# The unit of attention and indexer keys of a hybrid decoder trunk, multiplied in plain float32

## The chip, the cores and the metric

The program runs on one core of one Trainium2 chip. The metric is the device time of one execution in microseconds (us). TensorE (PE) multiplies matrices, VectorE (DVE) and ScalarE (ACT) work element by element, GpSimd (POOL) does small things, SyncE (SP) issues nearly all DMAs. Each engine runs its own instructions in order; semaphores join them.

## The reference, cut to what matters

Two layers over 256 tokens of width 1024, all float32. Each has a mixer and then a channel part (a dense SwiGLU in layer 0, top-2-of-8 experts in layer 1). The mixer's input projection is cut into segments:

```python
proj = h @ w_in
aq, ak, av, iq, ik, iw, bq, bk, bv, bg, ba = jnp.split(proj, _split_points(), axis=-1)
y_a = dsa_attention(aq, ak, av, iq, ik, iw * IDX_HEADS ** -0.5)   # indexer, top-k keys, softmax
log_a = jax.nn.log_sigmoid(ba @ w_a2 + b_a) / GATE_TAU
o = gla(bq, bk, bv, log_a)                                        # gated linear attention
y = jnp.concatenate([y_a, rms_norm(o, gla_g) * silu(bg)], axis=-1) @ w_out
```

`ak` (64 wide) are the attention keys, `ik` (64) the indexer keys, `av` (64) the attention values, `iw` (8) the indexer's head weights. The change concerns these four.

## The kernel before, in words

The program is written by hand, one list of instructions for each engine (`block.sync`, `block.gpsimd`, `block.scalar`, `block.tensor`, `block.vector`), so the order in the source is the order on each engine.

**Units.** The input projection is loaded and multiplied in 12 units of up to 256 columns (`W_IN_UNITS`: BQ, BA, BK, IQ0, IQ1, KEYS, AQ0, AQ1, BV0, BV1, BG0, BG1), the output projection in 4 more. A unit of weights lands in one of four buffers `u_raw` (L419, issued by SP). The first two units (`PLAIN`) are multiplied as they are, in float32 (L984, L978), with `hfull`, the modulated tokens. The others are split: ACT copies the unit into `u_high` in the type float32r (`conv_unit`, L646), DVE subtracts that from the raw weights and writes the rest into `u_low` (`low_unit`, L1508), over the raw buffer; the tokens are split alike into `hT_H` and `hT_L`. `mm3` (L329 to L331) then makes each product out of three: high by high, low by high, high by low. There are three buffers `u_high`, taken in turn, so `conv_unit` waits until the unit three before has been multiplied.

**The unit KEYS** (number 5, `U_KEYS`) has 200 columns: `ak` and `ik` in columns 0 to 127, `iw` and `av` in 128 to 199. Only the first 128 are split (ACT L644, DVE L1506) and multiplied by `mm3`, 8 products of 128x256. The last 72 are multiplied in float32 by `mm4` (L932), which makes one product out of four column groups; these read the raw weights. ACT then copies the results out of PSUM (`evacuate`, L660 to L666); the copy of `iw` (L663) releases the indexer's products of queries and keys (`head_products`, L1034).

**Order around it.** On ACT: convert IQ1, `decay_in`, copy out BK, convert KEYS, `decay_out`, copy out IQ0, convert AQ0 (L646), `decay_keys` (L714, two exponentials of `kfac`), copy out IQ1, convert AQ1, copy out KEYS, then the indexer's relus (L753). On DVE: `decay`, `decay_keys` (L1595, L1598), the low part of KEYS (L1506), `decay_products` (L1607 to L1613; L1613 multiplies `kfac` and waits for the exponentials), the low parts of AQ0 and AQ1 (L1508), two rows of the conditioning matrix (`condition_rows`, L1495 and L1497), the indexer's sums (L1550, L1552), the selection by repeated maximum (L1566, L1567). On PE: BQ, BA, BK, IQ0, IQ1, KEYS, the indexer's products, the decay products (L932, L1081), AQ0, AQ1, the attention logits (L1034 with `akP`), and so on. On SP a unit's load waits until the unit four before has been multiplied; rows 66 and 67 (6 and 7 in layer 0) of the conditioning matrix and the load of BV1 wait for KEYS.

Of the kernel before, what the change touches and what calls it, by code (L numbers as in the profile page):

```python
# [17 lines left out]
F32 = mybir.dt.float32  # L18
# [56 lines left out]
PLAIN = 2  # L75
NSPLIT = NU - PLAIN
KW = 200
# [28 lines left out]
def hybrid_decoder(nc, x, c, w_in, w_a2, b_a, gla_norm_g, w_out, w_mod, b_mod, ln_g, ln_b,  # L106
# [3 lines left out]
    with ctx:  # L110
# [512 lines left out]
        def _(act):  # L623
# [11 lines left out]
            def conv_unit(l, u):  # L635

                act.wait_ge(w_ld[u % 4], unit_landed(l, u))
                if u >= PLAIN + 3:
                    act.wait_ge(s["proj"], l * NU + u - 2)
                elif l:  # L640
                    act.wait_ge(s["f_gu"], 2 * (STEPS - 1))
                dst, src = u_high[(u - PLAIN) % 3], u_raw[u % 4]
                if u == U_KEYS:
                    A(dst[:, :, 0:P], src[:, :, 0:P], ACT.Copy).then_inc(s["wH"], 1)  # L644
                else:
                    A(dst[:], src[:], ACT.Copy).then_inc(s["wH"], 1)  # L646

# [82 lines left out]
            def mixer(l):  # L730
# [9 lines left out]
                evacuate(l, U_BK)  # L740
                conv_unit(l, U_KEYS)
                decay_out(l)
# [182 lines left out]
        def _(pe):  # L925
# [45 lines left out]
            def project(l, u):  # L971
                b = bank[4 + u % 2]
                if u < PLAIN:
# [13 lines left out]
                    return  # L987
                WH, WL, W = u_high[(u - PLAIN) % 3], u_low[u % 4], u_raw[u % 4]
                pe.wait_ge(s["wL"], l * NSPLIT + u - PLAIN + 1)
                if u == PLAIN:  # L990
                    pe.wait_ge(s["hT_L"], 4 * l + 2)
                pe.wait_ge(s["evac"], l * NIN + u - 1)
                if u in (U_BV0, U_BV1, U_BG0, U_BG1):
                    for t in range(TT):
                        tok = slice(t * P, (t + 1) * P)
                        for kt in range(KT):
                            last = mm3(b[:, t * 256:(t + 1) * 256], hT_H[:, kt, tok], hT_L[:, kt, tok],
                                       WH[:, kt, :], WL[:, kt, :], kt == 0, kt == KT - 1)
                else:
                    for ct in range(1 if u == U_KEYS else 2):  # L1000
                        cc = slice(ct * P, (ct + 1) * P)
                        for kt in range(KT):
                            last = mm3(b[:, ct * T:(ct + 1) * T], WH[:, kt, cc], WL[:, kt, cc],
                                       hT_H[:, kt, :], hT_L[:, kt, :], kt == 0, kt == KT - 1)
                    if u == U_KEYS:
                        for t in range(TT):
                            for kt in range(KT):
                                last = mm4(b[:, T + t * 72:T + (t + 1) * 72], hfull[:, kt, t * P:(t + 1) * P], W[:, kt, P:KW],
                                           start=(kt == 0), stop=(kt == KT - 1))
                last.then_inc(s["proj"], 1)  # L1010

            def project_out(l, i, kts):

                u, v = NIN + i, W_OUT_ORDER[i]
                pe.wait_ge(s["wL"], l * NSPLIT + u - PLAIN + 1)
                WH, WL = u_high[(u - PLAIN) % 3], u_low[u % 4]
                for t in range(TT):
# [385 lines left out]
        def _(dve):  # L1403
# [97 lines left out]
            def low_unit(l, u):  # L1501

                dve.wait_ge(s["wH"], l * NSPLIT + u - PLAIN + 1)
                H, L, src = u_high[(u - PLAIN) % 3], u_low[u % 4], u_raw[u % 4]
                if u == U_KEYS:
                    V.tensor_tensor(L[:, :, 0:P], src[:, :, 0:P], H[:, :, 0:P].bitcast(F32), ALU.subtract).then_inc(s["wL"], 1)  # L1506
                else:
                    V.tensor_tensor(L[:], src[:], H[:].bitcast(F32), ALU.subtract).then_inc(s["wL"], 1)  # L1508

# [142 lines left out]
            def mixer(l):  # L1652
# [17 lines left out]
                decay_keys(l)  # L1670
                low_unit(l, U_KEYS)
                decay_products(l)
# [297 lines left out]
```

## Time and profile before

| | |
|---|---|
| median of 3 runs | 1322.58 us (1322.08 to 1323.61) |
| the profiled execution's own time | 1323.89 us |
| its span (first to last instruction) | 1322.2 us |
| mean granted TensorE clock | 0.975 of full speed |
| busy: PE, DVE, ACT | 1212.8, 552.1, 312.4 us |
| mixer of layer 1, from its transposes to its last product | 392.6 to some 523 us |

A profile shows one execution. Busy shares are means over stages with different limits: the experts of layer 1 (from about 555 us on) fill PE, while the mixers go back and forth between the engines. What a change in a mixer is worth is read from the waits of that place: which of the engines is waited for last.

### The profile page before, as it was taken

The numbers are of one execution on the slowest core, as the hardware profiler recorded it, in microseconds if no ns is written. First come the engines' busy times: TensorE is split into PE (matmuls) and PEld (weight loads), VectorE is DVE, ScalarE is ACT, GpSimd is POOL, SyncE is SP. The second block draws the span as 40 slices with busy tenths as digits, with TensorE's granted clock in tenths as the row PEclk, the third lists the DMA queues.
The fourth block names the chain that finished last, engine by engine and source line by source line (L and its number), as shares of the span: only waits on it lengthen the run. The fifth ranks groups of instructions, "written<-read, shape, count | busy, mean of one in ns | idle before, by whom it ended". The sixth has DMA issues, their size and how long they took to land.

```text
span 1322.2 us, 26435 instructions
## 1 busy us (share of the span) xinstructions
PE 1212.8 (92%) x11284; PEld 657.5 (50%) x11284; DVE 552.1 (42%) x841; ACT 312.4 (24%) x545; POOL 43.5 (3%) x84
## 2 busy tenths in 40 slices
PE   2988979999979887699999999999999999999996
PEld 1878867778858877423333333334333333333332
DVE  6898877777658997520021020020110210200224
ACT  0556133443236560220020020011110201200200
POOL 3100010000010000100000000000000000000001
PEclk9999979999989999799999999999999999999998
DMA  9954767899617549588999989989989989989850
GB/s 341 314 193 160 256 227 287 314 358 322 231 50 219 183 153 379 217 318 351 411 334 406 364 305 415 413 324 404 375 306 411 402 335 383 390 351 411 339 224 32
DMA packets 149083, 403.60 MB, mean 305 GB/s; under 512 B 19964, under 2 KB 71328, under 8 KB 137696
## 3 DMA queue, kind: packets, MB, share of 16 engines
q1 hardware_dynamic: 146720, 395.16, 79.9%
q0 software_dynamic: 2240, 6.68, 1.4%
q8 instruction: 92, 1.51, 0.5%
q14 instruction: 31, 0.25, 0.0%
HBM read 400.75 MB, written 1.05 MB: 304 GB/s over the span
## 4 chain that ended last, share of the span: by engine, by line
PE 67%; DVE 9%; issue 2%; DMA 1%; ACT 1%; POOL 0%; DVEq 0%; SPq 0%; ACTq 0%
PE bank L1284 34%; PE bank L1308 17%; PE bank L329 3%; PE bank L331 3%; PE bank L330 3%; PE bank L1318 2%; PE bank L1264 1%; DVE u_low L1508 1%; PE bank L1289 1%; DVE mod_acc L1497 1%; PE bank L1272 1%; DMA raw_u<-in_ffn_w_up_dram 1%; PE bank L1273 1%; PE bank L984 1%; DVE score L1567 1%
## 5 line engine op out<-in xcount | busy, mean ns | idle before, releaser
L1284 PE MATMUL bank<-raw_w,xg 128*32 128x512 f32 x4096 | 457.8, 593 | 1.1 <-issue 1.1
L1284 PEld LDWEIGHTS bank<-raw_w,xg 128*32 128x32 f32 x4096 | 126.7, 109 | 260.4 <-issue 258.2
L1308 PE MATMUL bank<-raw_w,heT 128*32 128x512 f32 x2112 | 232.9, 593 | 0.0
L1859 DVE TENSOR_TENSOR he<-he,bank 128x256 f32<-128x256 f32 x64 | 23.3, 417 | 384.5 <-ACT he L843 384.5
L1308 PEld LDWEIGHTS bank<-raw_w,heT 128*32 128x32 f32 x2112 | 66.9, 110 | 148.8 <-issue 147.6
L843 ACT ACTIVATE he<-bank 128x256 f32<-128x256 f32 (+1 forms) x72 | 21.4, 370 | 413.1 <-PE bank L1284 282.2
L1886 DVE SCALAR_TENSOR_TENSOR ycat<-bank,gate_tab,ycat 128x512 f32<-128x512 f32 x36 | 25.4, 747 | 184.7 <-PE bank L1273 182.8
L1497 DVE SCALAR_TENSOR_TENSOR mod_acc<-mod_row,c_act,mod_acc 128x1024 f32<-128x1024 f32 x70 | 89.9, 1284 | 9.6 <-DMA mod_row<-in_w_mod_dram 3.9
L329 PE MATMUL bank<-u_high,hT_H 128*128 128x256 f32 x256 | 75.1, 293 | 4.6 <-DVE u_low L1508 4.6
L331 PE MATMUL bank<-u_high,hT_L 128*128 128x256 f32 x256 | 72.8, 284 | 0.0
L330 PE MATMUL bank<-u_low,hT_H 128*128 128x256 f32 x256 | 72.7, 284 | 0.0
L329 PE MATMUL bank<-gu_H,hT_H 128*128 128x512 f32 x160 | 64.8, 405 | 0.0
L646 ACT ACTIVATE u_high<-u_raw 128x2048 fp32r<-128x2048 f32 x26 | 49.7, 1911 | 63.7 <-DMA u_raw<-in_w_in_dram 43.7
L331 PE MATMUL bank<-gu_H,hT_L 128*128 128x512 f32 x160 | 63.2, 395 | 0.0
L330 PE MATMUL bank<-gu_L,hT_H 128*128 128x512 f32 x160 | 63.1, 394 | 0.0
L1508 DVE TENSOR_TENSOR u_low<-u_raw,u_high 128x2048 fp32r<-128x2048 f32 x26 | 59.0, 2287 | 9.5 <-ACT u_high L646 9.3
L850 ACT ACTIVATE heT<-bank 128x512 f32<-128x512 f32 x24 | 14.3, 597 | 192.2 <-PE bank L1318 192.2
L1870 DVE TENSOR_TENSOR y_sum<-y_sum,bank 32x512 f32<-32x512 f32 x48 | 32.9, 686 | 62.1 <-ACT y_sum L867 61.6
L329 PEld LDWEIGHTS bank<-u_high,hT_H 128*128 128x128 f32 x256 | 49.1, 192 | 7.4 <-DVE u_low L1508 5.9
L329 PE MATMUL bank<-hT_H,u_high 128*128 128x256 f32 x176 | 50.6, 287 | 1.5 <-DVE u_low L1506 1.5
L331 PE MATMUL bank<-hT_H,u_low 128*128 128x256 f32 x176 | 49.6, 282 | 0.0
L330 PE MATMUL bank<-hT_L,u_high 128*128 128x256 f32 x176 | 49.5, 281 | 0.0
(292 smaller groups left out, 1497.8 us busy)
## 6 DMA issues: line engine op xcount, KB each, us to landing
raw_w<-in_moe_w_down_dram SPq DMA_DIRECT2D x88, 1024.0 KB, 8.3
raw_w<-in_moe_w_gate_dram SPq DMA_DIRECT2D x128, 512.0 KB, 7.3
raw_w<-in_moe_w_up_dram SPq DMA_DIRECT2D x128, 512.0 KB, 8.6
mod_row<-in_w_mod_dram SPq DMA_DIRECT2D x80, 512.0 KB, 6.6
raw_w<-in_moe_w_gate_dram SPq DMA_DIRECT2D x64, 384.0 KB, 3.8
raw_w<-in_moe_w_up_dram SPq DMA_DIRECT2D x64, 384.0 KB, 5.0
u_raw<-in_w_in_dram SPq DMA_DIRECT2D x20, 1024.0 KB, 7.8
raw_d<-in_ffn_w_down_dram SPq DMA_DIRECT2D x11, 1024.0 KB, 9.9
```

Of the source, the lines that this page charges most:

```text
L329: nc.tensor.matmul(out_ap, aH, bH, start=first, stop=False)
L330: nc.tensor.matmul(out_ap, aH, bL, start=False, stop=False)
L331: return nc.tensor.matmul(out_ap, aL, bH, start=False, stop=last)
L646: A(dst[:], src[:], ACT.Copy).then_inc(s["wH"], 1)
L1284: last = mm(bank[m // 4][32 * q:32 * q + 32, :].rearrange("s (m f) -> s m f", m=2), xg[:, i, k, 32 * g:32 * g + 32], W[:, :, a * 256:(a + ...
L1308: last = mm(bank[3 + g][32 * q:32 * q + 32, :], heT[:, i, at:at + 32], W[:, b, h * 512:(h + 1) * 512], start=(c == 0 and a == 0), stop=(c ...
L1318: last = nc.tensor.transpose(o, rows, ident[:])
L1497: last = V.scalar_tensor_tensor(out=acc, in0=row[:], scalar=c_act[:, k:k + 1], in1=acc, op0=ALU.mult, op1=ALU.add)
L1508: V.tensor_tensor(L[:], src[:], H[:].bitcast(F32), ALU.subtract).then_inc(s["wL"], 1)
L1859: last = V.tensor_tensor(he[:, b, :], he[:, b, :], bank[b][:, 256:512], ALU.mult)
L1870: last = V.tensor_tensor(a, a, bank[3 + g][64 * h + 32:64 * h + 64, :], ALU.add)
L1886: V.scalar_tensor_tensor(out=a, in0=bank[b][:], scalar=gate_tab[:, t, bass.ds(E, 1)], in1=a, op0=ALU.mult, op1=ALU.add).then_inc(s["m_acc" ...
```

## The change

KEYS is no longer split. ACT and DVE lose their two instructions for it in each layer, PE multiplies its first 128 columns in float32 from `u_raw` and `hfull`, and waits for the landing of the weights instead of for `u_low`. The remaining split units are numbered by their place in the list `SPLIT`, which sets which `u_high` buffer each takes and which product `conv_unit` waits for. The copies out of PSUM, the 72 other columns and all DMAs stay.

```diff
-NSPLIT = NU - PLAIN
+SPLIT = [u for u in range(PLAIN, NU) if u != U_KEYS]
+NSPLIT = len(SPLIT)
...
                 act.wait_ge(w_ld[u % 4], unit_landed(l, u))
-                if u >= PLAIN + 3:
-                    act.wait_ge(s["proj"], l * NU + u - 2)
+                if SPLIT.index(u) >= 3:
+                    act.wait_ge(s["proj"], l * NU + SPLIT[SPLIT.index(u) - 3] + 1)
                 elif l:
                     act.wait_ge(s["f_gu"], 2 * (STEPS - 1))
-                dst, src = u_high[(u - PLAIN) % 3], u_raw[u % 4]
-                if u == U_KEYS:
-                    A(dst[:, :, 0:P], src[:, :, 0:P], ACT.Copy).then_inc(s["wH"], 1)
-                else:
-                    A(dst[:], src[:], ACT.Copy).then_inc(s["wH"], 1)
+                dst, src = u_high[SPLIT.index(u) % 3], u_raw[u % 4]
+                A(dst[:], src[:], ACT.Copy).then_inc(s["wH"], 1)
...
                 evacuate(l, U_BK)
-                conv_unit(l, U_KEYS)
                 decay_out(l)
...
-                WH, WL, W = u_high[(u - PLAIN) % 3], u_low[u % 4], u_raw[u % 4]
-                pe.wait_ge(s["wL"], l * NSPLIT + u - PLAIN + 1)
+                if u == U_KEYS:
+                    W = u_raw[u % 4]
+                    pe.wait_ge(w_ld[u % 4], unit_landed(l, u))
+                    pe.wait_ge(s["evac"], l * NIN + u - 1)
+                    for kt in range(KT):
+                        mm(b[:, 0:T], W[:, kt, 0:P], hfull[:, kt, :], start=(kt == 0), stop=(kt == KT - 1))
+                    for t in range(TT):
+                        for kt in range(KT):
+                            last = mm4(b[:, T + t * 72:T + (t + 1) * 72], hfull[:, kt, t * P:(t + 1) * P], W[:, kt, P:KW],
+                                       start=(kt == 0), stop=(kt == KT - 1))
+                    last.then_inc(s["proj"], 1)
+                    return
+                WH, WL = u_high[SPLIT.index(u) % 3], u_low[u % 4]
+                pe.wait_ge(s["wL"], l * NSPLIT + SPLIT.index(u) + 1)
...
-                if u == U_KEYS:
-                    V.tensor_tensor(L[:, :, 0:P], src[:, :, 0:P], H[:, :, 0:P].bitcast(F32), ALU.subtract).then_inc(s["wL"], 1)
-                else:
-                    V.tensor_tensor(L[:], src[:], H[:].bitcast(F32), ALU.subtract).then_inc(s["wL"], 1)
+                V.tensor_tensor(L[:], src[:], H[:].bitcast(F32), ALU.subtract).then_inc(s["wL"], 1)
...
                 decay_keys(l)
-                low_unit(l, U_KEYS)
                 decay_products(l)
```

How the instructions stand now is shown at two places. First, PE at the unit KEYS of layer 0, before: the end of its products out of high and low parts (`u_high_185`, `u_low_182`; eight such triples), the 72 other columns (`32x72 x64`), and the indexer's products behind them.

```order
L329 MATMUL bank<-hT_H,u_high_185 128x256
L330 MATMUL bank<-hT_L,u_high_185 128x256
L331 MATMUL bank<-hT_H,u_low_182 128x256
L932 MATMUL bank<-u_raw_178,hfull 32x72 x64
L1034 MATMUL bank<-ikP,iqT 128x128 x8
L1034 MATMUL bank<-ikP,iqT 128x256 x8
L932 MATMUL bank<-qfP,kfac 32x2x32 x64
```

The same place in the changed kernel: the last product of IQ1, then KEYS from `hfull` and the raw weights.

```order
L330 MATMUL bank<-hT_H,u_high_187 128x256
L331 MATMUL bank<-hT_L,u_high_187 128x256
L332 MATMUL bank<-hT_H,u_low_181 128x256
L990 MATMUL bank<-hfull,u_raw_178 128x256 x8
L929 MATMUL bank<-u_raw_178,hfull 32x72 x64
L1038 MATMUL bank<-ikP,iqT 128x128 x8
L1038 MATMUL bank<-ikP,iqT 128x256 x8
L929 MATMUL bank<-qfP,kfac 32x2x32 x64
```

Of 24 instructions 8 are left, and they no longer read what DVE wrote; all behind them stands as it did.

Second, DVE in layer 0, from `decay_keys` to the low parts of AQ0 and AQ1, before:

```order
L1595 TENSOR_TENSOR kfac<-bT 128x1024
L1598 TENSOR_SCALAR kfac<-kfac 128x1024
L1506 TENSOR_TENSOR u_low_182<-u_raw_178,u_high_185 128x8x128
L1607 TENSOR_TENSOR qfP<-bqT,dec_117 64x2x256
L1608 TENSOR_TENSOR qxP<-bqT,dec_118 64x2x128
L1607 TENSOR_TENSOR qfP<-bqT,dec_117 64x2x256
L1608 TENSOR_TENSOR qxP<-bqT,dec_118 64x2x128
L1609 TENSOR_TENSOR kx<-kx,bkT 128x256
L1613 TENSOR_TENSOR kfac<-kfac,bkT 128x1024 x2
L1508 TENSOR_TENSOR u_low_183<-u_raw_179,u_high_186 128x2048
L1508 TENSOR_TENSOR u_low_184<-u_raw_180,u_high_187 128x2048
```

And in the changed kernel:

```order
L1596 TENSOR_TENSOR kfac<-bT 128x1024
L1599 TENSOR_SCALAR kfac<-kfac 128x1024
L1608 TENSOR_TENSOR qfP<-bqT,dec_117 64x2x256
L1609 TENSOR_TENSOR qxP<-bqT,dec_118 64x2x128
L1608 TENSOR_TENSOR qfP<-bqT,dec_117 64x2x256
L1609 TENSOR_TENSOR qxP<-bqT,dec_118 64x2x128
L1610 TENSOR_TENSOR kx<-kx,bkT 128x256
L1614 TENSOR_TENSOR kfac<-kfac,bkT 128x1024 x2
L1509 TENSOR_TENSOR u_low_183<-u_raw_179,u_high_185 128x2048
L1509 TENSOR_TENSOR u_low_184<-u_raw_180,u_high_186 128x2048
```

The subtraction of KEYS is gone and AQ0 takes the buffer `u_high_185`, which was that of KEYS; the order of the rest is the same.

## Rows read from the trace of the kernel before

**Rows 1.** The page, part 4: shares of the span in the chain of waits, by engine

```profile
PE 67%; DVE 9%; issue 2%; DMA 1%; ACT 1%; POOL 0%; DVEq 0%; SPq 0%; ACTq 0%
```

**Rows 2.** The chain of waits from 380 to 560 us: start, us, what

```profile
423.38 1.22 DVE u_low L1506
...
477.49 4.30 DMA mod_row<-in_w_mod_dram
...
549.52 5.89 PE bank L1264 x32
```

**Rows 3.** Timeline of PE, layer 1: start, us, engine, line, names [idle before <- releaser]

```profile
423.03 0.28 PE L331 MATMUL bank<-hT_H,u_low 128*128 128x256 f32 x1
...
424.65 0.39 PE L329 MATMUL bank<-hT_H,u_high 128*128 128x256 f32 x1 [1.34 <-DVE u_low L1506]
...
427.70 2.21 PE L932 MATMUL bank<-u_raw,hfull 128*32 128x72 f32 x128
```

**Rows 4.** Timeline of PE, dense part of layer 0

```profile
184.20 3.62 PE L1187 MATMUL bank<-raw_u,hfull 128*128 128x256 f32 x16
...
187.65 3.62 PE L1187 MATMUL bank<-raw_g,hfull 128*128 128x256 f32 x16
```

**Rows 5.** Timeline of PE, layer 0

```profile
64.62 0.39 PE L329 MATMUL bank<-hT_H,u_high 128*128 128x256 f32 x1 [0.20 <-DVE u_low L1506]
```

**Rows 6.** Timeline of ACT, layer 0

```profile
57.84 1.06 ACT L644 ACTIVATE u_high<-u_raw 128x1024 fp32r<-128x1024 f32 x1 [2.01 <-DMA u_raw<-in_w_in_dram]
...
64.57 1.92 ACT L646 ACTIVATE u_high<-u_raw 128x2048 fp32r<-128x2048 f32 x1 [2.07 <-DMA u_raw<-in_w_in_dram]
...
66.39 1.99 ACT L714 ACTIVATE kfac<-kfac 128x1024 f32<-128x1024 f32 x2
...
68.76 1.90 ACT L646 ACTIVATE u_high<-u_raw 128x2048 fp32r<-128x2048 f32 x1
...
70.69 0.38 ACT L660 ACTIVATE ikP<-bank 64x256 f32<-64x256 f32 x1
```

**Rows 7.** Timeline of ACT, layer 1

```profile
423.60 1.91 ACT L646 ACTIVATE u_high<-u_raw 128x2048 fp32r<-128x2048 f32 x1 [1.54 <-DMA u_raw<-in_w_in_dram]
...
425.42 1.99 ACT L714 ACTIVATE kfac<-kfac 128x1024 f32<-128x1024 f32 x2
...
429.97 0.38 ACT L660 ACTIVATE ikP<-bank 64x256 f32<-64x256 f32 x1 [0.28 <-PE bank L932]
...
432.20 0.60 ACT L753 ACTIVATE relu_a<-bank 128x512 f32<-128x512 f32 x1 [0.32 <-PE bank L1034]
```

**Rows 8.** Timeline of DVE, layer 1

```profile
426.92 2.35 DVE L1613 TENSOR_TENSOR kfac<-kfac,bkT 128x1024 f32<-128x1024 f32 x2
...
429.19 4.49 DVE L1508 TENSOR_TENSOR u_low<-u_raw,u_high 128x2048 fp32r<-128x2048 f32 x2
...
435.65 0.28 DVE L1550 TENSOR_SCALAR score<-relu_a,iw 128x128 f32<-128x128 f32 x1
```

**Rows 9.** Timeline of DVE, layer 0

```profile
67.46 2.36 DVE L1613 TENSOR_TENSOR kfac<-kfac,bkT 128x1024 f32<-128x1024 f32 x2 [0.48 <-ACT kfac L714]
```

**Rows 10.** Windows: stretch, length, busy us by engine, granted clock, DMA share, GB/s

```profile
176.20:181.60 5.40, 5.40 (x21) 5.04 (x22) 4.20 (x9) 1.52 (x2) 0.00 (x0) 0.50 1.08 370
...
392.60:396.60 4.00, 4.00 (x18) 3.91 (x19) 2.88 (x7) 0.94 (x1) 3.23 (x6) 0.50 0.43 142
...
397.00:400.00 3.00, 3.00 (x16) 2.64 (x15) 3.00 (x4) 2.54 (x2) 0.00 (x0) 1.00 0.00 0
...
549.50:553.80 4.30, 4.28 (x20) 4.30 (x21) 2.79 (x13) 0.98 (x2) 1.81 (x1) 0.50 0.00 0
```

**Rows 11.** Windows, mixer of layer 1

```profile
486.00:489.00 3.00, 0.81 (x13) 0.53 (x16) 2.93 (x9) 2.99 (x7) 0.00 (x0) 1.00 0.95 321
...
489.50:492.00 2.50, 2.50 (x107) 2.50 (x101) 2.47 (x4) 1.13 (x1) 0.00 (x0) 0.50 0.01 4
...
492.50:495.00 2.50, 1.84 (x16) 1.60 (x17) 2.47 (x5) 1.24 (x3) 0.00 (x0) 1.00 0.52 126
```

More of the change, by code:

```diff
@@ L999, in project @@
                 else:
-                    for ct in range(1 if u == U_KEYS else 2):
+                    for ct in range(2):
                         cc = slice(ct * P, (ct + 1) * P)
@@ L1004, in project @@
                                        hT_H[:, kt, :], hT_L[:, kt, :], kt == 0, kt == KT - 1)
-                    if u == U_KEYS:
[L1006 to L1009, printed above, removed]
                 last.then_inc(s["proj"], 1)
@@ L1014, in project_out @@
                 u, v = NIN + i, W_OUT_ORDER[i]
-                pe.wait_ge(s["wL"], l * NSPLIT + u - PLAIN + 1)
-                WH, WL = u_high[(u - PLAIN) % 3], u_low[u % 4]
+                pe.wait_ge(s["wL"], l * NSPLIT + SPLIT.index(u) + 1)
+                WH, WL = u_high[SPLIT.index(u) % 3], u_low[u % 4]
                 for t in range(TT):
@@ L1501, in low_unit @@
             def low_unit(l, u):
-                dve.wait_ge(s["wH"], l * NSPLIT + u - PLAIN + 1)
-                H, L, src = u_high[(u - PLAIN) % 3], u_low[u % 4], u_raw[u % 4]
-                if u == U_KEYS:
-                    V.tensor_tensor(L[:, :, 0:P], src[:, :, 0:P], H[:, :, 0:P].bitcast(F32), ALU.subtract).then_inc(s["wL"], 1)
-                else:
-                    V.tensor_tensor(L[:], src[:], H[:].bitcast(F32), ALU.subtract).then_inc(s["wL"], 1)
+                dve.wait_ge(s["wH"], l * NSPLIT + SPLIT.index(u) + 1)
+                H, L, src = u_high[SPLIT.index(u) % 3], u_low[u % 4], u_raw[u % 4]
+                V.tensor_tensor(L[:], src[:], H[:].bitcast(F32), ALU.subtract).then_inc(s["wL"], 1)
             def layer_norm(ph, terms):
```

## The prediction

> **What bounds the kernel now.** I read the chain of waits first, because busy shares mix stages. Over the whole span it is mostly PE [rows 1], which is the expert part; but in the mixer of layer 1 it runs through DVE, and the subtraction that the change removes is a piece of it: 1.22 us from 423.38 on [rows 2]. Further on it goes through a DMA of conditioning rows at 477.49 and through PE's gathers at 549.52 [rows 2], and from there PE works on without a gap worth the name into the experts. The chain as printed does not reach back to the mixer of layer 0, so there I read the timelines of the engines and ask the same question: who is waited for last.
>
> **PE's part of the change.** In each layer 24 matrix products in float32r go and 8 in float32 come. Before, KEYS occupied PE in layer 1 from 424.65 until the 72 other columns began at 427.70, which is 3.05 us for the 24 [rows 3], some 0.13 us each. The float32 product of the same size stands in the dense part of layer 0: 16 records, two to a product, from 184.20 to 187.65 [rows 4], so 3.45 us for 8 products. The new KEYS therefore costs PE 3.45 - 3.05 = 0.40 us more in each layer. In its favour, the wait for the subtraction goes. In layer 1 the last product of IQ1 started at 423.03 and KEYS at 424.65, with 1.34 us put down to the subtraction [rows 3]; now it can start at about 423.16, and its last part ends at 423.16 + 3.45 + 0.1 for the change of type + 2.21 = 428.9 instead of 429.9. In layer 0 the wait was 0.20 us [rows 5]; KEYS starts about 0.35 us earlier there and ends about 0.1 us later.
>
> Neither is on the path. In layer 0 ACT comes to the copies of KEYS only at 70.69, right behind the conversion of AQ1 (68.76 + 1.90 = 70.66) [rows 6]; KEYS ended at 64.62 + 3.05 + 2.21 = 69.9 and now ends at 70.0, so 0.6 us of cover are left. In layer 1 ACT waited 0.28 us for PE, until 429.97 [rows 7]; it now starts at 429.69. The relus are then ready from 432.2 + 0.6 = 432.8 us on, while DVE first takes one at 435.65 [rows 7, 8]: 2.8 us of cover, under which PE's price would have to grow sevenfold before it counted. I cost PE's part at nothing. If that cover were gone it would be +0.40 us a layer less the wait removed.
>
> **ACT's part.** One conversion of 1.06 us goes in each layer (57.84 in layer 0 [rows 6]). Behind it ACT waits for something else before it comes to what DVE needs: for the load of AQ0, 2.07 us until 64.57 in layer 0 [rows 6] and 1.54 us until 423.60 in layer 1 [rows 7]. That load is issued behind the product of BK and nothing of the change stands ahead of it. So the time gained turns into a longer wait for that DMA: worth nothing. The looser wait of `conv_unit` (AQ0 for BK instead of IQ0, AQ1 for IQ0, BV0 for IQ1) changes nothing either, since in ACT's order the copy of the product it waited for stands ahead of the conversion or the DMA comes later. The loads of BV1 and of two conditioning rows wait for KEYS, and move by -1.0 and +0.1 us with it; both are used many us later.
>
> **DVE's part, the only one on the chain.** The subtraction of 1.22 us goes in each layer. Right behind it stand the five decay products and then the multiplication of `kfac`, which waits for ACT's exponentials.
>
> - Layer 0: before, that multiplication already waited, 0.48 us, for the first exponential and began at 67.46 [rows 9]; ACT began the exponentials at 66.39, right after the conversion of AQ0, which waited for its load [rows 6]. This does not move. All of the 1.22 us turns into wait: the gain is 0.
> - Layer 1: the exponentials began at 425.42 [rows 7]. With the distance that layer 0 shows, 67.46 - 66.39 = 1.07 us, the first is there for DVE at 426.49. DVE began the multiplication at 426.92 [rows 8]; without the subtraction its products end at 425.8, so it now waits until 426.49. The gain is 426.92 - 426.49 = 0.43 us, and the other 0.8 us become a wait for ACT, behind it for the load of AQ0.
>
> What is late next in layer 1 is again DVE: two subtractions, the conditioning rows and the indexer follow without a gap until 435.65 and beyond [rows 8]. The DMA of rows at 477.49 is released by DVE's reading of an earlier row, so it moves along. I carry 0.43 us to the start of the gathers.
>
> **What the clock takes of it.** PE idles before the expert part, and at 549.5 it starts at half clock, 1.2 GHz: granted 0.50 up to 553.8 [rows 10]. The rise to 2.4 GHz does not keep one distance from PE's restart: at 176.2 PE restarts and has 0.50 still 5.4 us later, at 392.6 it restarts and has 1.00 from 397.0 on, after 4.4 us [rows 10]. So I take it that the rise keeps its instant when PE restarts 0.43 us sooner, and the extra 0.43 us are run at half clock and worth 0.22 us. If the rise moved with the restart, all 0.43 us would arrive. The Trainium skill ("TensorE: Matmul & The Clock Gate", section "What's actually happening") says of the monitor behind the clock that it is free-running, "it doesn't reset when your kernel starts"; by that rule the sum is -0.22 us, without it -0.43 us, and the unequal distances above agree with it.
>
> **The sum.** Layer 0: 0. Layer 1: -0.43 us, of which 0.22 us reach the end. Against the profiled execution's own 1323.89 us that is 1323.7. The median of the three runs is 1.3 us lower than that execution, and I set the change against the median: 1322.58 - 0.22 = 1322.4 us. About 0.2%, or 2.6 us, is what a measurement of this kernel can tell from no change; this lies far below.
>
> **The rivals.**
>
> 1. *The whole subtraction counts* (chance 0.12). If AQ0's load came in earlier, or ACT's exponentials were not what DVE meets next, DVE would gain 1.22 us in layer 1, perhaps in both. For it: the subtraction stands in the chain of layer 1 in full [rows 2]. Against it: ACT's waits for that DMA stand in both layers, and layer 0 shows DVE waiting for the exponentials already. Times: 1322.58 - 1.22 = 1321.4, for both layers 1320.1.
> 2. *The clock falls behind KEYS* (chance 0.14, on the other side). PE has less to do around KEYS and, in layer 1, idles longer behind it, from 428.9 to about 430.7 instead of from 429.9 to 431.0. Gaps of that kind can bring the clock down: around 486 to 489 PE is busy for 0.81 of 3.0 us, and then it works at half clock [rows 11]. If the clock fell behind KEYS, the attention's units AQ0 and AQ1 or the products ahead of them would run part of their time at 1.2 GHz. Half clock holds there from 489.5 to 492.0 and full clock stands before 489.0 and after 492.5 [rows 11], so 2.5 to 3.5 us; at half speed that costs up to 1.7 us, if nothing hides it. It decides from where PE's delay passes the time DVE spends in the first selection. Against it: in both layers the present gaps of 1.1 to 1.8 us behind KEYS leave the clock at full. Times: 1322.4 + 1.7 = 1324.1 for one layer, 1325.8 for both, and only the latter (0.04) is beyond what can be told from no change.
> 3. *Nothing arrives* (chance 0.08). The wait of 4.30 us for the conditioning rows [rows 2] could be set by the queue and not by DVE's reading; then 0.43 us vanish in it. Time: 1322.6.
>
> **How the numbers follow.** The forecast has 0.66; its own range is 1321.6 to 1323.2, since the three runs differ by 1.5 us and the clock's instants differ between executions. The range for 8 in 10 takes in the third rival, the first for one layer and the second for one layer: 1321.0 to 1324.2. Left out are both layers of the first (0.04) and of the second (0.04) and chance shifts. Faster by over 0.2% is below 1319.9: 0.02. Slower by over 0.2% is above 1325.2: 0.04. Within: 0.94.
>
> **What would show it.** Right: in layer 1 the multiplication of `kfac` waits for ACT's exponential for about 0.7 us and starts 0.4 us earlier against the conversion of AQ0; in layer 0 it starts at the same distance as before, with about 1.7 us of wait instead of 0.48; KEYS has 16 records of float32 at 0.216 us; the copies of KEYS in layer 0 do not wait for PE. Wrong: half clock between KEYS and AQ1, PE named as the releaser of the relus or of the logits where it was not, or a load of AQ0 that lands at another distance from the product of BK.

## The result, and the profile after

The changed kernel is **slower by 1.0%**: 1335.75 us, the median of four runs (1333.9 to 1337.39), against 1322.33 us, the median of four runs of the kernel before (1319.13 to 1323.61). The ratio is 1.0101, with a 95% interval of 1.0079 to 1.0123. The forecast was 1322.4 us, and its whole range of 1321.0 to 1324.2 us lies below what was measured.

| | before | after |
|---|---|---|
| profiled execution, us | 1323.89 | 1335.46 |
| span, us | 1322.2 | 1333.7 |
| instructions | 26435 | 26397 |
| PE busy, us | 1212.8 | 1218.4 |
| DVE busy, us | 552.1 | 550.1 |
| ACT busy, us | 312.4 | 310.4 |
| granted clock of PE, mean | 0.975 | 0.970 |

What was to go has gone: DVE and ACT each have two instructions and 2 us less. Of PE's, 16 weight loads and 16 products have gone, and its busy time rose by 5.6 us. The groups of instructions say where. The gate and up products of the experts on the page of before, and on that of after (busy us, mean ns | idle before them and what ended it):

```profile
L1284 PE MATMUL bank<-raw_w,xg 128*32 128x512 f32 x4096 | 457.8, 593 | 1.1 <-issue 1.1
```

```profile
L1288 PE MATMUL bank<-raw_w,xg 128*32 128x512 f32 x4096 | 464.1, 600 | 6.4 <-issue 6.4
```

The same 4096 records take 6.3 us more, and there are 5.3 us more of idle ahead of them, which no other engine and no DMA ended: "issue" is what the profile writes when PE waited for nothing that it shows. Together that is 11.6 us. The edit does not touch these products.

Where in the experts it happens is seen in the timeline of PE. The experts' code is a loop of PE over pairs of experts, `with nc.Fori(0, n_last, ..., hint_back_edge=True)` (L1383 before, L1387 after), run three times, and then one pair written out behind it. Each pass begins with 48 gate and up products behind six transposes. Before, at the head of passes 1, 2 and 3 and of the pair behind the loop:

```profile
578.97 5.36 PE L1284 MATMUL bank<-raw_w,xg 128*32 128x512 f32 x48 [0.22 <-issue]
...
766.78 5.36 PE L1284 MATMUL bank<-raw_w,xg 128*32 128x512 f32 x48 [0.50 <-issue]
...
954.51 5.36 PE L1284 MATMUL bank<-raw_w,xg 128*32 128x512 f32 x48 [0.42 <-issue]
...
1141.74 5.36 PE L1284 MATMUL bank<-raw_w,xg 128*32 128x512 f32 x48
```

The same rows after:

```profile
579.04 7.01 PE L1288 MATMUL bank<-raw_w,xg 128*32 128x512 f32 x48 [0.21 <-issue]
...
771.07 8.27 PE L1288 MATMUL bank<-raw_w,xg 128*32 128x512 f32 x48 [3.06 <-issue]
...
964.38 7.05 PE L1288 MATMUL bank<-raw_w,xg 128*32 128x512 f32 x48 [3.10 <-issue]
...
1153.31 5.36 PE L1288 MATMUL bank<-raw_w,xg 128*32 128x512 f32 x48
```

The two kernels reach the first pass 0.07 us apart and leave the loop 11.57 us apart, which is the whole difference of the spans (11.5 us). It has two parts. The idle at the heads of passes 2 and 3 grew from 0.50 to 3.06 and from 0.42 to 3.10 us: 5.2 us. And the 48 products behind it, always 5.36 us before, took 7.01, 8.27 and 7.05 us: 6.3 us. The windows of after at these places show why (stretch, length, busy us of PE, PEld, DVE, ACT and POOL, granted clock, DMA share, GB/s):

```profile
579.00:586.00 7.00, 6.96 (x49) 1.68 (x49) 4.22 (x7) 4.80 (x10) 0.00 (x0) 0.76 0.57 200
...
771.00:779.20 8.20, 8.13 (x48) 1.92 (x48) 4.18 (x7) 2.29 (x4) 0.00 (x0) 0.64 0.36 122
779.20:789.00 9.80, 9.80 (x86) 3.24 (x86) 0.57 (x1) 0.38 (x1) 0.00 (x0) 1.00 0.88 284
964.30:971.40 7.10, 7.02 (x49) 1.92 (x49) 4.15 (x7) 2.27 (x4) 0.00 (x0) 0.76 0.40 132
```

A mean of 0.64 or 0.76 is a stretch that is partly at half clock (1.2 GHz); from 779.2 us on it is 2.4 GHz again. Before, the same places are at 1.00; this is the second:

```profile
766.70:772.10 5.40, 5.32 (x49) 1.54 (x49) 3.97 (x6) 3.67 (x7) 0.00 (x0) 1.00 0.99 368
```

What PE waited for is not in these views, since they count no branches. It is in the answer for the loop's own line, with the instructions of PE's queue (shortest/median/longest ns, first and last start), before:

```profile
L1383 PEldq COMPARE_BRANCH  x3: 88/3542/3622, 762.9 to 1138.4; - x3
```

and after:

```profile
L1387 PEldq COMPARE_BRANCH  x3: 88/6178/6212, 764.6 to 1150.0; - x3
```

The branch that closes a pass is taken twice and fallen through once (88 ns). The two that are taken last 3.5 to 3.6 us before and 6.2 us after. The difference between a branch's duration and PE's idle is the same in both: 3.5 to 3.6 us less 0.4 to 0.5, and 6.2 us less 3.1, which is 3.1 us each time. So PE has about 3.1 us of products queued when its sequencer meets the branch, and what lasts longer becomes idle.

What the sequencer waits for is seen among the DMA queues. Queue 8 is of the kind "instruction". In the 3.7 us behind the branch (764.6 to 768.3 us) the changed kernel moves 209 packets, and none of that queue; then, from 768.2 to 768.6 us:

```profile
q8 instruction: 1, 0.02, 15.8%
```

Before, that one packet comes in the stretch from 763.9 to 764.4 us, behind a branch at 762.9:

```profile
q8 instruction: 1, 0.02, 11.0%
```

In both, PE's sequencer goes on 2.5 us after this packet: its first instruction of the next pass, the hint on the branch, stands at 770.9 us after and at 766.6 us before. What lies between packet and sequencer is as long as it was; the packet comes 3.75 us behind the branch instead of 1.2 us. That it carries the loop's head is argued from this, not read: the view doesn't say what a packet holds. At the third branch, which is fallen through, a packet follows too, 0.8 us behind it before and 4.6 us after, and PE does not wait.

That gives the theory for the experiments. **Theory A**: PE's program is fetched in pieces, and what the closing branch costs depends on its place in them. The change took 16 weight loads and 16 products, 32 instructions, out of PE's program ahead of the loop, and so moved the branch. By the packets, a piece is 1.51 MB / 92 = 16 KB, and PE's 11284 weight loads and 11284 products before, in pieces of 256, would be 88 of the 92. The Trainium skill ("Runtime: NRT & Kernel Launch", section "Instruction fetch mechanics") gives the same 16 KiB and 256 instructions for a piece, and says that fetching ahead is sequential and that a taken branch to a piece that isn't held waits for a fetch. **Theory B**: the change itself slows the experts, by the state in which it leaves the clock, the queues or the DMAs. **Theory C**: it is the instant at which PE reaches the loop.

### The profile page after: what moved, and what is told of

Read it like the earlier page. It is cut to its first block, busy times and chain, and to the rows that moved or that the text cites. A ratio compares the mean times of both kernels' runs of the same rounds, so it can differ in the third digit from the quotient of the medians.

```text
span 1333.7 us, 26397 instructions
## 1 busy us (share of the span) xinstructions
PE 1218.4 (91%) x11268; PEld 658.2 (49%) x11268; DVE 550.1 (41%) x839; ACT 310.4 (23%) x543; POOL 43.7 (3%) x84
## 3 DMA queue, kind: packets, MB, share of 16 engines
HBM read 400.75 MB, written 1.05 MB: 301 GB/s over the span
## 4 chain that ended last, share of the span: by engine, by line
PE 67%; DVE 8%; issue 2%; DMA 2%; ACT 1%; POOL 0%; DVEq 0%; SPq 0%; ACTq 0%
PE bank L1288 34%; PE bank L1312 17%; PE bank L330 3%; PE bank L332 3%; PE bank L331 3%; PE bank L1322 2%; PE bank L1268 1%; DVE u_low L1509 1%; PE bank L1293 1%; DVE mod_acc L1501 1%; PE bank L1276 1%; DMA raw_u<-in_ffn_w_up_dram 1%; PE bank L1277 1%; PE bank L981 1%; DVE score L1568 1%
## 5 line engine op out<-in xcount | busy, mean ns | idle before, releaser
L1288 PE MATMUL bank<-raw_w,xg 128*32 128x512 f32 x4096 | 464.1, 600 | 6.4 <-issue 6.4
L644 ACT ACTIVATE u_high<-u_raw 128x2048 fp32r<-128x2048 f32 x26 | 49.7, 1912 | 62.5 <-DMA u_raw<-in_w_in_dram 42.5
L331 PEld LDWEIGHTS bank<-u_low,hT_H 128*128 128x128 f32 x256 | 49.1, 192 | 0.7 <-issue 0.7
L332 PEld LDWEIGHTS bank<-u_high,hT_L 128*128 128x128 f32 x256 | 49.0, 191 | 0.0
L330 PE MATMUL bank<-hT_H,u_high 128*128 128x256 f32 x160 | 46.5, 290 | 0.0
```

The source lines that it names most:

```text
L330: nc.tensor.matmul(out_ap, aH, bH, start=first, stop=False)
L331: nc.tensor.matmul(out_ap, aH, bL, start=False, stop=False)
L332: return nc.tensor.matmul(out_ap, aL, bH, start=False, stop=last)
L1288: last = mm(bank[m // 4][32 * q:32 * q + 32, :].rearrange("s (m f) -> s m f", m=2), xg[:, i, k, 32 * g:32 * g + 32], W[:, :, a * 256:(a + ...
```

## The experiments

All but one add nothing but small float32 products, whose result nobody reads. Most add them where PE idles at the program's start; this is the run with 8 of them:

```diff
             nc.tensor.transpose(bank[7][:, 0:P], stage[:], ident[:]).then_inc(s["stageT"], 1)
+            for _ in range(8):
+                mm(bank[5][0:32, 0:1], ones[:, 0:32], ones[:, 0:1], start=True, stop=True)
 
             def sum_chunk(acc, o):
```

Such a product is two weight loads and two products of PE, 4 instructions. That they cost nothing by themselves shows in the timeline of PE of the run with 64, the most that was tried: they take 7 us and PE then still waits 7.9 us for DVE.

```profile
9.10 6.99 PE L956 MATMUL bank<-ones 128*32 128x1 f32 x128
23.99 1.04 PE L932 MATMUL bank<-ones,ycat 128*32 128x1 f32 x64 [7.90 <-DVE ycat L1431]
```

The measurements of all runs, with the place of the closing branch counted in instructions from where the changed kernel has it. "Taken" is the duration of the two taken branches, "idle" what PE idles at the heads of passes 2 and 3 ahead of or among the 48 products, by the profile. The kernel before was run beside each group on the same chip; its medians there were 1323.37 us (the four with 32, 224, 256 and 16 instructions), 1323.68 (the four with 32 in the body, 32 and 224, 40, and 128), 1321.82 ("before + 8" and the three below it), and 1319.38 us in one run beside the last three.

| kernel | branch moved by | taken, us | idle, us | median, us | ratio to before |
|---|---|---|---|---|---|
| after | 0 | 6.18, 6.21 | 3.06, 3.10 | 1335.75 | 1.0101 [1.0079, 1.0123] |
| before | 32 | 3.62, 3.54 | 0.50, 0.42 | 1322.33 | 1 |
| after + 16 | 16 | 4.16, 4.56 | 1.12, 1.52 | 1325.72 | 1.0022 [1.0007, 1.0038] |
| after + 32 | 32 | 3.26, 3.30 | 0.19, 0.19 | 1323.56 | 1.0023 [1.0007, 1.0039] |
| before + 256 | 32 + 256 | 3.20, 3.22 | 0, 0.17 | 1323.44 | 0.9999 [0.998, 1.0018] |
| before + 224 | 256 | 5.89, 5.96 | 2.77, 2.85 | 1334.7 | 1.0104 [1.0071, 1.0137] |
| after, 32 in the body | 32 | 3.06, 3.30 | 0, 0.19 | 1326.9 (one run) | |
| after + 32, 224 in the body | 256 | 6.22, 6.10 | 3.11, 2.99 | 1346.33 (one run) | |
| after + 40 | 40 | 2.86, 3.20 | 0, 0 | 1322.09 | 0.9989 [0.9973, 1.0005] |
| after + 128 | 128 | 0.41, 0.37 | 0, 0 | 1323.19 | 1.0 [0.9985, 1.0015] |
| before + 8 | 40 | 3.26, 3.36 | 0, 0.25 | 1322.73 | 1.001 [0.9994, 1.0025] |
| after + 40, again | 40 | 2.90, 3.42 | 0, 0.31 | 1322.24 | 1.0001 [0.9986, 1.0015] |
| after + 192 | 192 | 0.41, 0.37 | 0, 0 | 1325.21 | 1.0028 [1.001, 1.0046] |
| after, no hint | -1 | 6.19, 6.28 | 2.99, 3.07 | 1334.39 | 1.0107 [1.0074, 1.014] |
| after + 208 | 208 | 0.41, 0.37 | 0.28, 0 | 1326.3 (one run) | |
| after + 224 | 224 | 0.41, 0.37 | 0.74, 1.05 | 1327.76 (one run) | |
| after + 240 | 240 | 0.41, 0.40 | 0, 0 | 1329.01 (one run) | |

**After + 32: back to the old place.** The edit is the one above.

> The changed kernel with 8 small float32 products added on PE where it idles in the first 22 us; each becomes 4 records of PE, so 32 instructions come back ahead of the experts' loop, as many as the change took out of PE's program there. Theory A (what matters is where the loop's head and its branch lie in PE's program): the loop stands where it stood before, PE's idle at the first gate and up product of a later pass goes back from 3.1 us to 0.5 us, half clock there goes, and the time is 1322 us (1320 to 1324). Theory B (the change itself slows the experts, through the state in which it leaves the clock or the queues): the idle stays at 3.1 us and the time at 1335.5 us. Theory C (only the first pass depends on the instant of arrival): 1334.

Measured: 1323.56 us, 1.0023 of the kernel before beside it. In its timeline the heads of passes 2 and 3 read:

```profile
763.73 5.36 PE L1290 MATMUL bank<-raw_w,xg 128*32 128x512 f32 x48 [0.19 <-issue]
...
951.22 5.36 PE L1290 MATMUL bank<-raw_w,xg 128*32 128x512 f32 x48 [0.19 <-issue]
```

The whole change is in this kernel, and the loss is gone but for 0.2%, which the later runs with 40 instructions do not show. Theory B falls. So does theory C: PE reached the first pass 2.8 us sooner here than in the profile of after (576.25 for 579.04 us), but before and after had reached it within 0.07 us of each other and differ by the whole loss, and the run of before + 256 (580.60 us) reached it later and lost nothing.

**Before + 224: the new place without the change.** 56 small products instead of 8, in the kernel before.

> The kernel before with 56 small float32 products added on PE where it idles in the first 22 us: 224 instructions, which is 256 less the 32 that the change takes out. The subtraction and the float32r products of KEYS stay. Theory A, with PE's program fetched in pieces of 16 KB (256 instructions of 64 bytes): the loop stands in its pieces as in the changed kernel, PE idles 3.1 us at the head of passes 2 and 3, and the time is 1322.3 + 11.5 = 1334 us (1331 to 1337). If the place counts from the program's start and not within a piece: 1322 to 1324. Theory B (the change itself slows the experts): 1322.3 us, idle 0.5 us.

Measured: 1334.7 us, 1.0104, against 1.0101 for the change. Nothing of the change is in this kernel, and it has the whole loss, with the same rows:

```profile
768.84 6.86 PE L1286 MATMUL bank<-raw_w,xg 128*32 128x512 f32 x48 [2.77 <-issue]
...
960.49 8.31 PE L1286 MATMUL bank<-raw_w,xg 128*32 128x512 f32 x48 [2.85 <-issue]
```

**Before + 256: the control.** 64 small products.

> The control of the run beside it: the kernel before with 64 such products, 256 instructions, one whole piece of 16 KB. Theory A: the loop stands in its pieces as before, idle 0.5 us, 1322.3 us (1320.5 to 1324). If added work at the start costs by itself, or the distance from the program's start counts, the time is above 1325.

Measured: 1323.44 us, 0.9999. 224 more cost 11 us and 256 more nothing: the place counts within a stretch of 256 instructions, not from the start. The profile has 93 packets in queue 8 instead of 92, one piece more. This also excludes that added work at the start is what costs.

**After + 16: half of the way.** 4 small products.

> The changed kernel with 4 such products, 16 instructions: half of the way back. Theory A leaves open whether the stall falls in steps or evenly with the place of the loop: evenly would give an idle of about 1.8 us and 1328 to 1330 us, a step gives 1322 or 1335.5. Theory B: 1335.5.

Measured: 1325.72 us, taken branches of 4.16 and 4.56 us, idle of 1.12 and 1.52 us. The branch shortens with the place and not in one step, by some 0.11 us an instruction over the first 16 and 0.05 to 0.07 over the next 16; "evenly" had said an idle of 1.8 us. The time is 2.3 us below the 1328 expected; in its profile no head runs at half clock, all have their 5.36 us. An idle of 1.1 to 1.5 us left PE at 2.4 GHz in this place, and one of 2.8 to 3.1 us brought it to 1.2 GHz.

**The branch or the loop's head?** Both had moved together. The first run puts 32 instructions into the loop's body and none ahead of it, which moves the branch alone (and the second 32 ahead and 224 within, 28 instead of 4, which brings the branch round to the place in the changed kernel and the head to that of before):

```diff
                 pe.wait_ge(s["m_oS"], E + 1)
+                for _ in range(4):
+                    mm(bank[7][0:32, 0:1], ident[:, 0:32], ident[:, 0:1], start=True, stop=True)
                 for t in range(TT):
                     last = nc.tensor.transpose(bank[7][0:SLOTS, t * P:(t + 1) * P], one_G[:, t, :], ident[:])
```

> The changed kernel with 4 small float32 products of the identity in each expert, ahead of the transposes of the slots: 32 instructions more inside the loop, none ahead of it. The loop's head stays where the change put it, and its closing branch comes to where it stood before. If the branch's place decides, PE's idle at the first gate and up product of passes 2 and 3 falls from 3.1 to 0.2 to 0.5 us, and the time is 1335.7 - 11.5 + 0.9 x 4 = 1328 us (64 records more at 0.055 us are 0.9 us in each of 4 pairs at most). If the head's place decides, the idle stays near 3.1 us and the time is 1336 to 1339.

> The reverse: 32 instructions ahead of the loop and 224 inside it (28 small products in each expert), on the changed kernel. Within pieces of 256 instructions the head stands as in the kernel before and the closing branch as in the changed kernel. If the head decides: idle 0.2 to 0.5 us at the head of passes 2 and 3. If the branch decides: some 3 us. The time itself is above both kernels, by 56 products of 0.11 us, 6.2 us, in each of 4 pairs: 1347 us if the head decides, 1358 if the branch decides; only the idle is to be read.

Measured: the first 1326.9 us, with taken branches of 3.06 and 3.30 us and no idle at the head of pass 2; the second 1346.33 us, with 6.10 and 6.22 us:

```profile
772.09 6.75 PE L1290 MATMUL bank<-raw_w,xg 128*32 128x512 f32 x48 [3.11 <-issue]
...
967.24 8.15 PE L1290 MATMUL bank<-raw_w,xg 128*32 128x512 f32 x48 [2.99 <-issue]
```

Both say, each in one profile, that the place of the closing branch decides and that of the head does not. The time of the second was expected at 1358 us in this case; the small products inside cost less than the 0.11 us each that I had put, and only the idle was to be read from it.

**Farther along.** 10 and 32 small products, 40 and 128 instructions.

> The changed kernel with 10 small products on PE in the first 22 us: 40 instructions, 8 more than the kernel before has there. The idle fell evenly so far, from 3.1 us (none added) over 1.1 to 1.5 us (16) to 0.2 us (32). If it is the time in which the rest of a piece of 256 instructions is passed or fetched, this place is just over a piece's border and the idle is either none (0 to 0.2 us, 1323 us) or jumps to the whole piece's (many us: 1345 us or more).

> The changed kernel with 32 such products, 128 instructions. If the stall grows by 0.09 us for each instruction by which the loop stands ahead of the border (3.1 us more for 32), it would be about 14 us longer than at the best place for 160 instructions, and the time 1322 + 2 x 14 = 1350 us or more. If it grows only over the last 40 instructions and is flat elsewhere, idle is 3 us and the time 1335; if the bad stretch is only about the present place, 1323.

Measured: 1322.09 and 1323.19 us, no idle in either. With 40, the taken branches last 2.86 and 3.20 us, a little less than with 32. With 128 the account of an even growth falls: they last

```profile
L1389 PEldq COMPARE_BRANCH  x3: 88/365/410, 767.4 to 1141.8; - x3
```

0.4 us, and the packet of queue 8 is seen 6.7 us ahead of the branch (767.38 us), from 760.4 to 760.9 us:

```profile
q8 instruction: 1, 0.02, 14.6%
```

The next packet comes 3.8 us behind the branch, when PE's sequencer has long gone on. So there are places where the back edge waits for no packet behind it. That the head had come with the packet ahead of the branch is argued: the changed kernel has a packet ahead of its branch as well, by 10.9 us. The short branch gains nothing further here, since 3.0 us are covered anyway.

**Both kernels at the same good place.** The kernel before with 2 small products (8 instructions), and the changed kernel with 40 once more.

> The kernel before with 2 small products, 8 instructions: the loop's closing branch comes to the place within 256 instructions that it has in the run of the changed kernel with 40 more. At that place the fetch behind the branch came 0.4 to 0.8 us after it and PE did not idle. By the account of the branch's place the two kernels, so placed, differ by the mixer alone: this one 1322 to 1323 us, and the changed one 0 to 1 us less. If something of the change besides the place costs time, this one is faster by more than 1 us.

> The changed kernel with 10 small products, 40 instructions, once more beside the kernel before with 8: 1322 us (1321 to 1323), ratio to the kernel before 0.998 to 1.000. If it is faster than the kernel before by more than 1 us, idle of 0.2 to 0.5 us at the head of the loop and the 0.43 us of the mixer are not all of it.

Measured: 1322.73 and 1322.24 us; beside the kernel before, 1.001 and 1.0001, with intervals of 0.15% to each side. With the loop's place held equal, the medians differ by 0.5 us, with a 95% interval (resampled from the twelve runs of each) of some 2.5 us faster to 1.5 us slower: not told from nothing.

**64 ahead of the changed kernel's place, and without the hint.** The first has 48 small products; the second is the one kernel that adds none:

```diff
-            with nc.Fori(0, n_last, engines=[pe.engine], hint_back_edge=True) as pr:
+            with nc.Fori(0, n_last, engines=[pe.engine], hint_back_edge=False) as pr:
```

> The changed kernel with 48 small products, 192 instructions: the branch lies 64 instructions ahead of its present place. With 128 more the fetch came 6.7 us before the branch and PE's sequencer resumed 0.4 us behind it; at the present place (256 more) it comes 3.75 us after it. If the fetch's instant moves evenly with the place between these two, it comes between 1 us before and 1 us after the branch, and the sequencer resumes after 1.5 to 3.5 us, without idle of PE; 1322 to 1324 us. If the bad stretch is wider than the last 32 instructions: resume after 5 us and more, 1330 to 1340 us.

> The changed kernel with the hint on the back edge of PE's loop taken out (one instruction less in each pass, the branch lies one instruction earlier). If the hint starts the fetch at the present place, it comes later without it, and idle at the head of passes 2 and 3 grows from 3.1 us to 5 or more: 1340 us and more. If the hint does nothing at this place, as a fetch 3.75 us behind the branch suggests, 1335.7 us with the same idle. If it is the hint that delays the fetch, the idle falls and the time is 1323.

Measured: with 192, taken branches of 0.37 and 0.41 us and no idle, but 1325.21 us, 0.28% above the kernel before. Its profiled execution shows 1 us of these 3: the 48 products, 5.36 us where nothing holds them, take 5.48, 5.58 and 6.00 us at the heads of passes 2 and 3 and behind the loop. Where the rest goes was not found. Without the hint 1334.39 us and idle of 2.99 and 3.07 us: the hint does nothing at this place. Whether it is what makes the early fetch with 128 more, I did not try.

**Where the edge is.** With 192 more the branch waits 0.4 us, with 256 more (that is, 0) 6.2 us. Three single runs lie between: 52, 56 and 60 small products.

> The changed kernel with 52 small products, 208 instructions: the branch is 48 instructions ahead of its place in the changed kernel. If the wait is the passing of the rest of the piece (0.09 us an instruction) and this place is still on that side of the edge: 6.2 + 48 x 0.09 = 10.5 us from the branch to the resume, PE idle 7.4 us, 1350 us or more. If the edge lies behind it: resume after 0.4 us, no idle, 1322 to 1326 us.

> With 56 small products, 224 instructions, 32 ahead of its place in the changed kernel. Passing the rest of the piece: 6.2 + 32 x 0.09 = 9.1 us, idle 6 us, 1345 us. Behind the edge: 0.4 us, 1322 to 1326 us. Crest at the present place: between the two, 3 to 6 us, 1324 to 1334.

> With 60 small products, 240 instructions, 16 ahead of its place in the changed kernel. Passing the rest of the piece: 6.2 + 16 x 0.09 = 7.6 us, idle 4.5 us, 1340 us. Behind the edge: 0.4 us, 1322 to 1326 us.

Measured: 1326.3, 1327.76 and 1329.01 us, where the kernel before had 1319.38 us in its one run beside them. In all three the taken branches last 0.4 us, which was expected of an edge behind them. The account by which the sequencer passes the rest of the piece falls, and the edge lies within the last 16 instructions. But these kernels are not free of idle either; it sits elsewhere. With 240 there are 0.83 us at the head of pass 1, where the others have 0.2 to 0.3, and this at the pair behind the loop, where the branch is fallen through:

```profile
1145.31 6.92 PE L1290 MATMUL bank<-raw_w,xg 128*32 128x512 f32 x48 [3.28 <-issue]
```

and with 208 and 224 in the middle of the 48 products: 0.28 us in pass 2 and 0.47 us behind the loop with 208, and 0.74, 1.05 and 1.25 us in passes 2 and 3 and behind the loop with 224, of which this is the last:

```profile
1146.48 4.49 PE L1290 MATMUL bank<-raw_w,xg 128*32 128x512 f32 x37 [1.25 <-issue]
```

Each of these waits also ends behind a packet of queue 8. With 240, one comes from 1142.6 to 1143.1 us, 4.2 us behind the branch, and PE goes on 2.45 us after its start:

```profile
q8 instruction: 1, 0.02, 11.6%
```

The idles in the middle of the 48 products, with 208 and 224, end 2.3 to 2.6 us behind such a packet, which itself comes 3.6 to 4.2 us behind the branch. So the price has not gone at these places. It has moved from the back edge to the next piece that PE needs: this agrees with a head that was there in time and a piece behind it (behind the loop, the one that leaves it) that was not. Which piece each packet holds is again argued, not read.

## Why the prediction was wrong, step by step

**The step that failed** is a term that stood at nothing without a reason: the experts. The first part follows PE, "from there PE works on without a gap worth the name into the experts", and goes no further; and the part on PE costed 24 products out and 8 in by their durations around KEYS and left the rest of PE's program as it was. The edit has a second price there, for the 32 instructions themselves, at a branch that is first taken 340 us of run time behind KEYS of layer 1 (764.6 for 424.7 us): some 10 us of the 11.5 in the profiled executions. In the sum stood 0, and none of the rivals had it. The page could have warned: the 1.1 us of idle "<-issue" ahead of L1284 stood there, and the timeline puts them at the heads of the passes, 0.22, 0.50 and 0.42 us. Of the 3.6 us that the taken branch lasted, 3.1 were covered; the cover was used up, and whatever lengthened the branch had to count in full.

Its terms in the mixer, by the profile of after:

- **PE's part: the price right, the cover in layer 0 not.** KEYS was to take 3.45 us and takes 3.55 (64.96 to 68.51 us in layer 0, 421.17 to 424.72 in layer 1), and starts without a wait:

```profile
421.17 3.62 PE L990 MATMUL bank<-hfull,u_raw 128*128 128x256 f32 x16
424.72 2.21 PE L929 MATMUL bank<-u_raw,hfull 128*32 128x72 f32 x128
```

  In layer 0 it starts 0.34 us later than before, not 0.35 us earlier, and its last 72 columns end at 70.72 us. The 0.6 us of cover ahead of ACT's copies are gone: ACT is free at 70.22 us and waits 0.56 us for PE, which the prediction had named as not happening. It costs nothing, since the cover ahead of DVE held in both layers: DVE takes the first relu 3.3 us after ACT began it in layer 0 (76.29 for 73.01 us) and 3.2 us in layer 1 (432.37 for 429.22) [rows 7, 8].
- **ACT's part: right in what it is worth, not in what ACT waits for.** Without the conversion ACT waits longer for DVE's `dec` (3.00 us in layer 0, where it did not wait, and 2.53 for 1.58 in layer 1), and less for the load of AQ0: 1.73 us until 64.13, and 0.35 us until 420.26 [rows 6, 7].
- **DVE in layer 0: 0 forecast, 0.44 us measured.** The multiplication of `kfac` begins at 67.02 us instead of 67.46 [rows 9], as the load of AQ0 came 0.44 us sooner (64.13 for 64.57). It waits 0.81 us, not 1.7: besides the earlier load, DVE began `kfac` 0.36 us later (59.99 for 59.63). Two executions can't tell how much of this is the change.

```profile
67.02 2.36 DVE L1614 TENSOR_TENSOR kfac<-kfac,bkT 128x1024 f32<-128x1024 f32 x2 [0.81 <-ACT kfac L712]
```

- **DVE in layer 1: 0.43 us forecast, 1.14 us measured.** From the first of the last two subtractions for `kfac` (L1595) to the multiplication it was 7.27 us (419.65 to 426.92) and is 6.13 (417.50 to 423.63), without any wait: here the first rival's size is the right one.

```profile
417.50 1.22 DVE L1596 TENSOR_TENSOR kfac<-bT 128x1024 f32<-128x1024 f32 x1
...
423.63 2.36 DVE L1614 TENSOR_TENSOR kfac<-kfac,bkT 128x1024 f32<-128x1024 f32 x2
```

  In the run of after + 32 the same stretch is 6.89 us, with 0.68 us of wait for ACT behind a later load of AQ0: the forecast's case. So it depends on the load, and both occur. Over all profiles the first rival's size is the nearer: from the first transposes of layer 1 to DVE's first sum of the indexer it is 43.0 to 43.9 us in the four kernels without the change (mean 43.3) and 41.2 to 42.5 us in the thirteen with it (mean 41.9).
- **The way to the gathers: "it moves along" was wrong.** The prediction read the 4.30 us at 477.49 as a wait that DVE's earlier reading would move. In the profile before, DVE does not wait there; it works on from 476.18 to 484.49 us. In that of after it comes to these rows 3.28 us sooner (1.76 us of it because the layer began sooner) and waits for their DMA, which takes 6.63 us from 474.21 on, so that 0.94 us of the lead are left:

```profile
476.18 8.31 DVE L1497 SCALAR_TENSOR_TENSOR mod_acc<-mod_row,c_act,mod_acc 128x1024 f32<-128x1024 f32 x6
...
480.87 2.67 DVE L1501 SCALAR_TENSOR_TENSOR mod_acc<-mod_row,c_act,mod_acc 128x1024 f32<-128x1024 f32 x2 [2.51 <-DMA mod_row<-in_w_mod_dram]
```

  All thirteen profiles with the change have such a wait, of 0.2 to 2.8 us, the four without it 0 to 2.5 us. From the transposes of layer 1 to the gathers both kinds take the same, 158.2 us with the change and 158.4 us without in the mean, and single profiles differ by up to 4.7 us. That is the end of the third rival, "nothing arrives"; whether the queue sets the landing, as that rival had it, was not tried.
- **What arrives: 0.22 of 0.43 us forecast, nothing measured.** The gathers start 0.94 us sooner, at 548.58 us, and the experts' products behind them at 555.41 us, where it was 555.34 before. The records keep their length of 0.61 to 0.63 us, that of half clock, until the last one at 555.07 us, while half clock had ended by 553.87 us before [rows 10]: the rise to 2.4 GHz came 1.2 us later.

```profile
548.58 0.71 PE L1268 MATMUL bank<-one_P,xH 128*128 128x192 f32 x2 [4.04 <-DVE xL L1807]
...
555.07 0.41 PE L1268 MATMUL bank<-one_P,xL 128*128 128x192 f32 x2
555.41 2.78 PE L1288 MATMUL bank<-raw_w,xg 128*32 128x512 f32 x24
```

  That the clock swallows a part was right, that the rise keeps its instant was not. Between executions this matters little beside what else varies: over all the profiles PE reaches the first pass between 576.15 and 583.44 us, with the change or without.
- **The clock behind KEYS (rival 2)** did not fall. The clock did fall, but behind the loop's branch.

The forecast for the mixer, -0.22 us, is not contradicted by the two kernels at equal place (1322.24 and 1322.73 us), but that is in part luck: DVE's gain in layer 1 was put too small and the share that arrives too large. The error of 13 us is the missing term: the changed kernel moved by 40 instructions has none of it (1322.09 and 1322.24 us).

Of the 6.3 us at half clock in the profile of after, 1.65 belong to pass 1, ahead of any taken branch. They come and go from one execution to the next: the two profiles of after + 40 have 5.36 us there in one and 7.05 in the other. So some 10 us are the branch's, 5.2 as idle and 4.6 as half clock behind it.

## What to carry to other kernels

A kernel with a long loop on a busy engine can have a term that no line of a diff shows: instructions added or removed anywhere ahead of it move its closing branch within the pieces in which the program is fetched, and here 32 of them made each back edge 2.6 us longer, which the clock then nearly doubled. Before costing such a change, read how long the branch lasts (its own line in the trace) against the idle behind it; where idle "<-issue" stands at a loop's head the cover is used up, and a few instructions either way count. When a result comes out wrong in a place that the edit doesn't touch, add instructions to the old kernel until its code stands where the new one's does: it separates the edit from its place in one run, and the cure is the same padding (the changed kernel with 40 instructions more runs in 1322.1 us, as fast as the kernel before and no faster). A short branch alone does not prove a good place: with 224 and 240 instructions more the branch took 0.4 us and PE idled elsewhere. And a gain in the middle of a chain has to be followed to its end: DVE's 1.4 us were gone by the gathers, behind waits for a DMA.

## What the runs showed of the hardware

- The taken branch lasts 6.2 us at the worst place that was met, 4.2 to 4.6 us 16 instructions farther, 3.2 to 3.6 at 32, 2.9 to 3.4 at 40 and 0.4 us from 128 to 240; 224 and 256 instructions in the kernel before gave what the period of 256 says (5.9 and 3.2 us).
- Where the branch or a piece behind it was waited for, PE's sequencer went on 2.3 to 2.6 us behind a packet of queue 8. What sets the instant of that packet, 0.4 to 3.8 us behind a taken branch that waits, stays open.
- The rule on branches of the Trainium skill ("Runtime: NRT & Kernel Launch", section "Instruction fetch mechanics") agrees with the taken branches of 2.9 to 6.3 us, each of which ends behind a packet. It does not give those of 0.4 us.
- Where the back edge was free, PE could idle elsewhere instead: 3.28 us on leaving the loop with 240 more, 0.7 to 1.25 us among the first 48 products with 224 more.
- At the heads of passes 2 and 3 and behind the loop, an idle of 0.7 to 1.5 us left PE at 2.4 GHz; one of 2.8 to 3.3 us was followed by 1.2 GHz for part of the next 7 to 8 us, which cost 1.4 to 3 us more each time.
